# Layer 1 reordered: queries first, sample 0's keys under the gated values, each head mixed in its own pass, value pages on SyncE's queue

## What is computed

```python
h = rms_norm(x, norm_g) * (1.0 + scale) + shift
qc, kc, vc, gc, ud, vd, gd = split_cols(h @ w_in, ODD_SIZES)      # seven times 1024 columns
qc, kc = rms_norm(heads(qc), q_norm_g), rms_norm(heads(kc), k_norm_g)
oc = stick_breaking_sweep(qc, k_all, v_all, n_past, sb_offset) * silu(gc)
vn = rms_norm(gelu(vd), v_norm_g)
od = gelu(ud) * (w @ vn + b_s) * silu(gd)         # w: lower triangle of 128 x 128, per group
y = x + gate * (concatenate([oc, od]) @ w_out)
```

## Time and profile before

| | us |
|---|---|
| median of 3 runs | 2480.41 |
| lowest, highest | 2479.94, 2484.56 |
| the profiled execution | 2479.76 |
| its span, first to last instruction | 2478.2 |
| TensorE busy in the span | 2238.9 (90%) |

### The profile page before, as it was taken

How to read it: one execution, slowest core, us unless ns; L and a number is a source line. 1 busy time by engine, 2 the same in 40 slices (tenths; PEclk the granted TensorE clock), 3 DMA queues, 4 the chain that set the end, 5 groups by cost and what they waited for, 6 DMA issues and landing times.

```text
span 2478.2 us, 46284 instructions
## 1 busy us (share of the span) xinstructions
PE 2238.9 (90%) x17191; PEld 1973.8 (80%) x17191; DVE 1166.4 (47%) x3560; ACT 596.7 (24%) x741; POOL 258.9 (10%) x429
## 2 busy tenths in 40 slices
PE   6799999999999999699979997999989889877997
PEld 2188888888888878599969997887777777755997
DVE  1543333424433342533453436767657657664332
ACT  1322121212212111222233331321321322222221
POOL 0000100101010010100000001112112112111110
PEclk9999999999999899699989998999999999988999
DMA  9977455554655555034332335778668668663442
GB/s 310 320 218 208 147 164 157 164 161 147 192 154 152 158 147 176 21 103 115 115 137 86 88 89 181 251 246 296 213 224 282 220 236 273 212 229 124 129 135 65
DMA packets 399987, 436.44 MB, mean 176 GB/s; under 512 B 16917, under 2 KB 306991, under 8 KB 399168
## 3 DMA queue, kind: packets, MB, share of 16 engines
q1 hardware_dynamic: 340838, 244.88, 33.1%
q0 software_dynamic: 49184, 180.78, 21.2%
q10 hardware_dynamic: 9810, 8.73, 1.0%
HBM read 407.79 MB, written 26.54 MB: 175 GB/s over the span
## 4 chain that ended last, share of the span: by engine, by line
PE 67%; DMA 11%; DVE 10%; issue 6%; ACT 3%; POOLq 2%; POOL 1%; ACTq 1%; DVEq 0%; SPq 0%
PE pt L465 52%; PE m L465 13%; DMA arena<-in_cache_k 7%; DVE arena L1553 3%; ACT arena L854 2%; DMA arena<-in_cache_v 1%; PE m L469 1%; POOLq L1759 1%; DMA raw<-in_e_w_ada 1%; ACT w_hi L854 1%; DMA arena<-in_o_k_norm_g 1%; DVE arena L1364 1%; PE pt L469 0%; DVE arena L1310 0%; DVE w_lo L1193 0%
## 5 line engine op out<-in xcount | busy, mean ns | idle before, releaser
L465 PE MATMUL pt<-act_hi,w_hi 128*128 128x260 f32 x4384 | 922.3, 292 | 54.4 <-DVE act_lo L1276 21.8
L465 PE MATMUL pt<-act_hi,w_lo 128*128 128x260 f32 x4384 | 896.1, 286 | 0.0
L465 PE MATMUL pt<-act_lo,w_hi 128*128 128x260 f32 x4384 | 896.1, 287 | 0.0
L465 PEld LDWEIGHTS pt<-act_hi,w_hi 128*128 128x128 f32 x4384 | 692.7, 194 | 118.7 <-issue 69.0
L1193 DVE TENSOR_TENSOR w_lo<-raw,w_hi 128x1024 fp32r<-128x1024 f32 x274 | 335.4, 1224 | 873.1 <-ACT w_hi L854 872.6
L465 PEld LDWEIGHTS pt<-act_lo,w_hi 128*128 128x128 f32 x4384 | 692.3, 193 | 0.0
L465 PEld LDWEIGHTS pt<-act_hi,w_lo 128*128 128x128 f32 x4384 | 690.2, 192 | 0.0
L854 ACT ACTIVATE w_hi<-raw 128x1024 fp32r<-128x1024 f32 x274 | 289.9, 1058 | 1297.7 <-PE pt L465 1283.4
L1553 DVE CUSTOM_DVE_ANT_0 arena<-arena 128x128 f32<-128x128 f32 x1024 | 225.9, 287 | 99.5 <-DMA arena<-in_cache_k 90.1
L465 PE MATMUL m<-arena 128*128 128x128 f32 (+7 forms) x1136 | 211.1, 347 | 10.5 <-POOL arena L1840 4.1
L854 ACT ACTIVATE arena<-arena 128x1040 f32<-128x1040 f32 (+8 forms) x199 | 169.1, 862 | 151.7 <-DVE arena L1670 52.3
(11 more groups left out here) (156 smaller groups left out, 1094.3 us busy)
## 6 DMA issues: line engine op xcount, KB each, us to landing
arena<-in_cache_k POOLq DMA_DIRECT2D x128, 512.0 KB, 4.9
arena<-in_cache_v POOLq DMA_DIRECT2D x128, 512.0 KB, 5.7
raw<-in_o_w_in SPq DMA_DIRECT2D x112, 512.0 KB, 4.3
raw<-in_e_w_in SPq DMA_DIRECT2D x98, 512.0 KB, 4.5
raw<-in_e_w_ada SPq DMA_DIRECT2D x96, 512.0 KB, 5.7
raw<-in_o_w_ada SPq DMA_DIRECT2D x96, 512.0 KB, 5.4
raw<-in_e_w_out SPq DMA_DIRECT2D x32, 512.0 KB, 3.9
raw<-in_o_w_out SPq DMA_DIRECT2D x32, 512.0 KB, 4.7
```

The lines of the kernel that those rows point to most:

```text
L465: return pe.matmul(out, lhsT, rhs, start=start, stop=stop, skip_group_check=True)
```

## The change

The table of tiles, the steps of all five engines in layer 1 and the place of the transfers are written anew. The arithmetic stays.

- `l1a`: its four rounds are straight code. The first two have the eight tiles of queries, the last two the eight of gated values. Thirty-six steps are counted through; the queries' norm stands at steps 4, 8, 13 and 17 and behind, the gated values' at 22, 26, 31 and 35, and VectorE scores the keys of sample 0 in steps 26 to 30 and 32 to 34.
- `l1b`: the tiles of a pass come as K, V, GD, U, G. Pass i mixes head i, reads the values of sample i and scores the keys of sample i+1, into one of two score arrays that take turns (the second lies in `mod[0]`). The key steps of a pass are 1, 3, 4, 5, 7, 8, 9, 10. The final product of head i with its gates, `gate`, comes in pass i+1 at step 2. Passes 1 to 6 are a loop of three rounds with two passes each.
- Value pages are loaded by SyncE between the weights' loads; GpSimd loads key pages, query rows and mixing weights.
- There is no pass without tiles. The gate of head 7 and the last rows' pick stand among the splits for the output projection, which takes input chunks 8 to 15 first (`TAKE1`, `OUT1_FIRST`).

```diff
-L0_TO, L1A_TO, L1B_TO = [0, 1, 3, 2, 4, 5], [0, 1, 2, 3], [4, 3, 2, 1, 0]
+L0_TO, L1A_TO, L1B_TO = [0, 1, 3, 2, 4, 5], [0, 1, 2, 3], [0, 1, 3, 4, 2]
+OUT1_FIRST = [(0, 1), (0, 0), (1, 0), (1, 1)]
+TAKE1 = [8, 9, 10, 11, 12, 13, 14, 15, 0, 1, 2, 3, 4, 5, 6, 7]
+
+
+Q_AT, V_AT = [4, 8, 13, 17], [22, 26, 31, 35]
+L1A_STEPS = 36
+KEYS0_AT = [26, 27, 28, 29, 30, 32, 33, 34]
+KEYS_AT = [1, 3, 4, 5, 7, 8, 9, 10]
...
+            def value_page(b, p):
+                first = isinstance(b, int) and b == 0
+                if p >= 3:
+                    sp.wait_ge(s("v_free"), b * 16 + (p - 2))
+                elif not first:
+                    sp.wait_ge(s("v_free"), b * 16 - (0, 2, 1)[p])
+                page = sp.value_load(ptab[0:1, bass.ds(b * NPAGE + p, 1)], min_val=0, max_val=NPOOL - 1)
+                sp.dma_start(pages[:, value_slot(p), :], cv[bass.ds(page, 1)].rearrange("n s d -> (n s) d"))\
+                    .then_inc(s(f"page{value_slot(p)}"), 16)
+
+            def l1b_pass(i, last=False):
+                for at_ in range(10):
+                    if at_ < 6:
+                        l1b_load(i, at_ + 4)
+                    elif not last:
+                        l1b_load(i + 1, at_ - 6)
+                    else:
+                        out1_load(at_ - 6)
+                    if at_ == 0:
+                        for p in (1, 2, 0):
+                            value_page(i, p)
+                    if at_ >= 3:
+                        for p in (2 * at_ - 3, 2 * at_ - 2):
+                            if p < NPAGE:
+                                value_page(i, p)
+
+            sp.wait_ge(s("ptab"), 16)
+            for u in range(4):
+                l1b_load(0, u)
+            l1b_pass(0)
+            with sp.Fori(1, 7) as i:
+                l1b_pass(i)
+            l1b_pass(7, True)
...
+            def mix1(i):
+                first = isinstance(i, int) and i == 0
+
+                yield
+                if not first:
+                    pick(i)
+                yield
+                pe.wait_ge(s("s_rest"), i + 1)
+                mm(M[3][:, 256:384], cm["from_key"][:, :], zsa, start=True, stop=False)
+                pe.wait_ge(s("s_later"), i + 1)
+                mm(M[3][:, 256:376], ones[:, :], later, start=False, stop=True).then_inc(s("s_sum"), 1)
+                yield
+                if first:
                     pe.wait_ge(s("vd_sq"), 4)
                     feature_sum(tmp[4], M[0], M[1][:, 0:8], "vd_ss")
...
+                value_pages(i, 0)
...
+                pe.wait_ge(s("k_sq"), i + 1)
+                if first:
+                    pe.wait_ge(s("rv"), 1)
+                else:
+                    pe.wait_ge(s("gated"), i)
+                pe.wait_ge(s("ws_in"), i * 32 + 32)
+                mm(M[0], ones[:, :], tmp[0][:, 0:T])
+                mm(M[1][:, 0:8], ones[:, :], tmp[0][:, T:N])
+                tr(M[2][:, 0:P], ws)
+                pe.wait_ge(s("vn"), i + 1)
+                tr(M[2][0:NB, P:2 * P], tmp[2][:, T:N]).then_inc(s("p0"), 1)
+                value_pages(i, 1)
...
+                value_pages(i, 7)
+                pe.wait_ge(s("weight"), i + 1)
+                for b in range(NT):
+                    mm(M[0][:, P * b:T], vtok1[:, b, :], za[:, SB_OFF[b]:SB_OFF[b] + T - P * b],
+                       start=(b == 0), stop=(b == 3))
+                for t in range(NT):
+                    mm(M[1][:, P * t:P * t + P], vntok[:, t, :], wst, start=True, stop=False)
+                    last = mm(M[1][:, P * t:P * t + P], ones[0:1, :], brow[0:1, 0:P], start=False, stop=True)
+                last.then_inc(s("oc"), 1)
...
+            l1b(0, 0)
+            with pe.Fori(0, 3) as n:
+                l1b(n * 2 + 1, 1)
+                l1b(n * 2 + 2, 0)
+            l1b(7, 1)
...
+            def l1a_mix():
+                for n in range(L1A_STEPS):
+                    for r in range(4):
+                        if n == Q_AT[r] + 2:
+                            dve.wait_ge(s("q_rs"), r + 1)
+                            for t in range(2):
+                                last = stt(wide[:, 2 * r + t, :], G[r % 2 * 2 + t], cols[:, C_QN:C_QN + 1], tmp[t],
+                                           ALU.mult, ALU.mult)
+                            step(last)
+                        value_gate(r, n - V_AT[r])
+                    if n == Q_AT[3] + 2:
+                        copy(qcol.rearrange("p (b h) -> p h b", b=NB), wide[:, 0:HC, T:N]).then_inc(s("q_col"), 1)
+                    if n in KEYS0_AT:
+                        key_pages(0, KEYS0_AT.index(n), zs[0])
+                    yield
...
+            def gate(n):
+
+                hd = n - 1
+                dve.wait_ge(s("g1_sig"), n)
+                tt(G[2], G[2], tmp[3], ALU.mult)
+                step(tt(G[3], G[3], tmp[4], ALU.mult))
+                step(tt(G[4], G[4], G[3], ALU.mult))
+                step(ts_(tmp[2][:, T:N], tmp[2][:, T:N], per_head[:, 1, bass.ds(hd, 1)],
+                         per_head[:, 2, bass.ds(hd, 1)], ALU.mult, ALU.add))
+                to = wide[:, bass.ds(hd + 8, 1), :].rearrange("p c n -> p (c n)")
+                copy(GS[:, bass.ds(hd, 1), :].rearrange("p c n -> p (c n)"), G[2][:, T:N])
+                tt(to[:, T:N], G[4][:, T:N], tmp[2][:, T:N], ALU.mult)
+                dve.wait_ge(s("oc"), n)
+                tt(to[:, 0:T], G[4][:, 0:T], M[1], ALU.mult)
+                tt(wide[:, bass.ds(hd, 1), 0:T].rearrange("p c n -> p (c n)"), G[2][:, 0:T], M[0], ALU.mult)\
+                    .then_inc(s("gated"), 1)
...
+                def keys(at):
+                    if at in KEYS_AT and not last:
+                        key_pages(i + 1, KEYS_AT.index(at), zn)
...
+                zv = zi.rearrange("p (g h) -> p g h", h=HC)
+                dve.wait_ge(s("k_free"), i * 16 + 16)
+                step(stt(zv, zv, SCALE, per_head[:, 0:1, :].to_broadcast([P, NPAGE, HC]), ALU.mult, ALU.add))
+                stt(zsa, zi, -1.0, zi, ALU.mult, ALU.max).then_inc(s("zs_abs"), 1)
+                if first:
+                    value_gate(3, 1)
+                else:
+                    rows_kept(i)
...
+                dve.wait_ge(s("s_sum"), i + 1)
+                tt(zi, zi, M[3][:, 256:384], ALU.subtract).then_inc(s("s_lw"), 1)
+                if first:
+                    value_gate(3, 3)
+                else:
+                    gate(i)
+                yield
+                copy(tmp[1], wide[:, bass.ds(i, 1), :].rearrange("p c n -> p (c n)"))
+                if not first:
+                    dve.wait_ge(s("gated"), i)
+                    v_normed()
+                keys(3)
...
+                keys(7)
+                dve.wait_ge(s("z_l"), i + 1)
+                step(stt(za, z, 0.0, za, ALU.max, ALU.add))
+                masks(za).then_inc(s("rest"), 1)
+                yield
+                keys(8)
+                dve.wait_ge(s("u_x2"), i + 1)
+                gelu_arg(tmp[0], G[4]).then_inc(s("u_u"), 1)
+                yield
+                dve.wait_ge(s("between"), i + 1)
+                tt(z, z, m012[:, 0:SB_ALL], ALU.subtract).then_inc(s("lw"), 1)
+                keys(9)
+                dve.wait_ge(s("w_e"), i + 1)
+                masks(za).then_inc(s("weight"), 1)
...
+            with dve.Fori(0, 3) as n:
+                step.body(n, 0, 24)
+                l1b(n * 2 + 1, 1)
+                l1b(n * 2 + 2, 0)
+            step.end(3, 24)
+            l1b(7, 1, True)
+            rows_kept(8)
+            dve.wait_ge(s("pe_tile"), tile_no("out1", 0, 0))
+            for n, c in enumerate(TAKE1):
+                if n == 4:
+                    gate(HC)
+                if c == 0:
+                    rows_picked(8)
+                    dve.wait_ge(s("mixed1"), HC)
+                    tt(wide[:, 0:HC, T:N], OS, GS, ALU.mult).then_inc(s("mixed1_all"), 1)
+                take(3, c, n)
...
+            def sample_keys(b):
+                for p in range(NPAGE):
+                    key_page(b, p)
+                    if p == 1:
+                        if isinstance(b, int) and b == 0:
+                            pool.wait_ge(s("q_out"), 16)
+                        queries(b)
+                        if not (isinstance(b, int) and b == 0):
+                            head_weights(b - 1)
+
+            sample_keys(0)
+            sample_keys(1)
+            with pool.Fori(2, NB) as b:
+                sample_keys(b)
+            head_weights(HC - 1)
```

714 lines of the change are left out of this document (309 added, 405 removed).

## The result

| | before | after |
|---|---|---|
| median, us | 2480.18 | 2441.41 |
| lowest, highest | 2475.9, 2484.56 | 2437.24, 2442.27 |
| span of the profiled execution | 2478.2 | 2440.2 |

The ratio is 0.984, with a 95% interval of 0.982 to 0.986: 1.6% faster, 39 us. The forecast was 2414.2 with a range of 2390 to 2462. Direction and range held; the time is 27 us above the forecast, so the gain is 39 us where 66 were expected. The rest of the text looks for these 27 us.

The account below looks back on a forecast made before the run. The prediction took TensorE, busy for 90% of the span, as the bound: 1462.7 + 2.1 + 18 + 8 x 87.5 + 9.4 + 3 + 208.6 + 8.8 = 2412.6 us of span, plus 1.6 is 2414.2. Range 2390 to 2462.

Parts of the forecast that it names:

- The tail without tiles: Last head's mixing and last sample's values with no tile beside them, layer 1: its 58.0 us go.
- Length of a pass: Each of eight layer 1 head passes takes 87.5 us, between bounds of 83.7 and 94.7.
- The straight pass: First head pass before the change, straight code: 87.0 us, TensorE busy 83.1; model for the 87.5 us pass.
- within 87.5 it costs about nothing: Key steps one unit apart in a pass: 8.1 us round trip, VectorE falls back 1.2 us, 3.5 us before TensorE notices.
- the rival of VectorE's pace: VectorE sets the pace of the passes, two later hand-overs cost 1.5 us each: pass 93 us, total 2458; chance 0.12.
- The prediction's own sign of being wrong: Passes over 90 us; TensorE then waits for in_cache_v, the split behind a key step, or in_cache_k with landings near 9 us.
- The turns: Two turns of the pass loop instead of five, VectorE late at each, TensorE idle 4.7 us: 9.4 us.
- Sample 0's keys: Key scoring moved under the gated values, steps 26 to 34: TensorE stands for 18 us, bounds 12 and 24.
- 1462.7 + 2.1 (query norm): Time up to the end of the sixteen query and gated-value tiles, plus 2.1 us for the fourth query head norm moved ahead.
- Pass 0: First head pass: the last gated pair's square sum falls into it, 2.1 us and a hand-over, 3 us.
- Value pages on SyncE's queue: Value page loads among weight loads: no weight late, three tight pages of 0.3 us each a pass, within the 87.5.
- The end: Behind pass 7, head 7's gates and the first output projection splits: 8.8 us, bounds 4 and 14.

Follow-up runs that it names:

- the kernel with one product: Changed kernel with VectorE computing one of the eight products of every key page, all pages still loaded, results not valid: 2397.15 us, ratio 0.963 to the kernel before.
- the first edit: Changed kernel with the second and fourth query norm one step later, at steps 9 and 18 for 8 and 17: ratio 0.977 to the kernel before.
- all four edits: Changed kernel with three key and two value buffers, query norms moved, sample 0's keys spread, passes 1 to 6 written out: 2381.84 us, ratio 0.957.

## Why the prediction was right and where it was not

**The tail without tiles, right.** The 58 us went whole. In pass 7, which has no keys to score, TensorE never waits (76.71 us of 76.71). The forecast gave that pass 87.5 like the others; the 5.0 us less were there to be had from the table of steps.

**Length of a pass: forecast 87.5 plus turns, 89.1 in the mean; measured 90.3 and 89.7.** Near, but partly by luck. The straight pass of the earlier trace rows was taken as a model with 3.9 us idle. A step that failed here is "within 87.5 it costs about nothing". The round trip of 8.1 us for a key slot was worked out there, and where sample 0's keys are scored it is what the chain shows. But it was worked out with the median landing of 5.0 us and then held against a slack of 3.5 us for the split alone. In the passes the slowest landing ahead of each long wait takes 7.5 to 8.1 us, a round trip of about 11 us (1.80 + 1.26 + 8); VectorE's longest single wait for a key page is 6.0 us, in place of 3.1 in the earlier trace rows. What is then late is not the split but `rest`, which the prediction priced only in the rival of VectorE's pace, at 1.5 us a hand-over. It is 3.9 us of idle TensorE a pass in the mean, and slow units behind it; with a third buffer it is 0. That the mean still came near 87.5 is luck: the straight pass taken as the model had 3.9 us of idle time too, of another kind. The prediction's own sign of being wrong, passes over 90 us, came true by a hair, and the line that TensorE waits for is none of the three that it named.

**The turns: right in number and near in size, wrong in the engine.** Two turns of 4.7 us were forecast. It is 3.75 and 3.35 us idle; with the slow units a turn is 5.75 us in the kernel with one product, where nothing else waits. They come from TensorE's own branch, and VectorE's stands ready behind it. The rows of before could not show TensorE's: there its branch takes 0.2 us.

**Sample 0's keys: 18 us forecast, 19.3 measured,** in part by the pace of about 8 us a step, where 7.3 was taken. What was not added is the low clock behind the waits, though the earlier trace rows held it: in the stretch with the same work before the change 542 matmuls took 73.6 us at a clock of 0.91, where the pace of the earlier trace rows gives 65.3.

**The largest failed step is "1462.7 + 2.1 (query norm)".** It took the first part over as it stood, and priced the moved norm by its matmuls and not by its place. In the new table two norms, the second and the fourth, stand at a seam with no unit between producer and user. That cost 13.2 us by the first edit, half of the 27. No row of the trace of before shows it, since there TensorE goes from tiles to the sum without a wait; the order of the new steps did.

**Pass 0: near.** 3 us were added to a pass that already held 3.9 us of idle time, so 6.9; measured are 7.6 (4.7 + 2.0 and three small ones), as VectorE has sample 0's last keys, its scores and the last gated pair in one step.

**The low clock, priced at nothing.** The 30.1 us up to the first pick can be worked out in full. The first weights of layer 1 are ready 2.3 us later. So the forecast, moved back to the earlier start, has its first norm at 1300.3 us and from there to the pick 1579.1 - 1300.3 = 278.8 us, 24.9 of them idle (18 + 3 + 3.9) and 253.9 busy; measured are 306.6, 35.2 and 271.4. The 10.3 us more of idle time are 8.3 at the seams, 1.3 at the keys and 0.7 in pass 0. Of the 17.5 us more of busy time the first edit takes back 5.2. The other 12.3 us are slower matmuls, mostly behind the waits for sample 0's keys and in pass 0, where the mean clock is 0.91 and 0.93 and not the 1.00 of the model. No run isolates these 12.3 us. But where the waits are few the same matmuls are quicker: with all four edits TensorE is busy for 260.7 us there.

**Value pages on SyncE's queue, right,** and of more weight than the prediction gave it: three tight pages of 0.3 us each were forecast, a wait of 0.2 us in six passes came, and with the values on GpSimd's queue in the interleaving tried here the new order is 6% slower than the kernel before.

**The end: 8.8 us forecast, 4.1 measured** (212.7 for 208.6). The wait for the first split is 2.02 us, not 3.5, and the gate of head 7 lies between two splits on VectorE's chain, from 2231.19 to 2234.94: 3.75 us, of which TensorE, with a unit to run, feels 1.0.

## What to carry to other kernels

When producers and users of several engines are put on a table of steps, look at the seams first, where two steps follow each other with no cover between. Price a ring of buffers by its round trip from free to landed, and with the slow landings too and not the median alone, against the pace of the steps; here one buffer more was worth more than any single move of a step. Give the time behind a wait of several us its price as well. And of two engines that stand at the same place for the same time, taking away one shows nothing: both must go.
